# Where TensorE's moving operand lies: high and low parts of the forms apart, or by turns tile by tile

## The reference

```python
z = rmsnorm(x, g_attn) @ w_in                                   # 2048 -> 4608
mix = concat([attention, memory attention, recurrence])          # 2048
x1 = x + mix @ w_out                                             # 2048 -> 2048
up = causal_dwconv3(rmsnorm(x1, g_ffn) @ w_up)                   # 2048 -> 12288
val, gate = split(up)
h = gelu(gate) * val                                             # 6144
y = x1 + h @ w_down                                              # 6144 -> 2048
```

## Time and profile before

| | |
|---|---|
| median of 3 runs | 2290.98 us (2290.85 to 2291.15) |
| the profiled execution, its own time | 2290.06 us |
| its span, first to last instruction | 2288.3 us |
| PE busy, matmuls | 2277.7 us, 17,856 |
| PEld busy | 2259.1 us |
| DVE, ACT, POOL busy | 1854.8, 1187.0, 287.5 us |
| DMA | 309.87 MB, mean 135 GB/s |

### The profile page before, as it was taken

One profiled execution on the slowest core, in us unless ns is written; L12 is line 12 of the kernel. 1 busy time (PEld: TensorE's weight loads), 2 busy tenths in 40 slices (PEclk: granted clock), 3 DMA queues, 4 the chain that ended last, 5 costly groups with the idle time before them and its releaser, 6 DMA issues.

```text
span 2288.3 us, 44911 instructions
## 1 busy us (share of the span) xinstructions
PE 2277.7 (100%) x17856; PEld 2259.1 (99%) x17856; DVE 1854.8 (81%) x2478; ACT 1187.0 (52%) x1911; POOL 287.5 (13%) x241
## 2 busy tenths in 40 slices
PE   9999999999999999999999999999999999999999
PEld 8999999999999999999999999999999999999999
DVE  6788667666888988888888888888888988787876
ACT  4566454444554555455555545555555555454643
POOL 4100000000011011121111111211211110000000
PEclk9999999999999999999999999999999999999999
DMA  9522422323345443444343343433445678686864
GB/s 292 156 76 73 125 85 83 112 80 90 113 145 175 114 122 118 119 128 128 110 136 119 117 138 110 139 117 119 136 120 152 169 199 205 162 209 160 218 145 102
DMA packets 479605, 309.87 MB, mean 135 GB/s; under 512 B 11176, under 2 KB 457640, under 8 KB 479416
## 3 DMA queue, kind: packets, MB, share of 16 engines
q1 hardware_dynamic: 470984, 289.97, 43.1%
q0 software_dynamic: 8432, 17.27, 4.5%
HBM read 255.79 MB, written 53.51 MB: 135 GB/s over the span
## 4 chain that ended last, share of the span: by engine, by line
PE 62%; DVE 2%; issue 1%; ACT 0%; DVEq 0%; ACTq 0%
PE out L2944 21%; PE out L2945 21%; PE out L2946 21%; DVE ring_l L2301 1%; DVE fl L2549 0%; ACT ring_h L1566 0%; DVE pair L2333 0%; DVE s_buf L2313 0%; DVE out L2404 0%; DVE pair L2340 0%; DVE pair L2323 0%; DVE ub L2532 0%; ACT fh L1743 0%; DVE ub L2360 0%; DVE stage L2357 0%
## 5 line engine op out<-in xcount | busy, mean ns | idle before, releaser
L2301 DVE TENSOR_TENSOR ring_l<-pair,ring_h 128x1024 fp32r<-128x1024 f32 (+1 forms) x384 | 455.0, 1185 | 176.2 <-ACT ring_h L1566 176.0
L1566 ACT CAST ring_h<-pair 128x1024 fp32r<-128x1024 f32 (+1 forms) x384 | 383.1, 998 | 323.0 <-DVE pair L2333 227.3
L2944 PE MATMUL out<-t,ring_h 128*128 128x272 f32 x1760 | 507.9, 289 | 2.3 <-DVE ring_l L2301 2.3
L2946 PE MATMUL out<-t,ring_l 128*128 128x272 f32 x1760 | 507.3, 288 | 0.0
L2945 PE MATMUL out<-t,ring_h 128*128 128x272 f32 x1760 | 505.1, 287 | 0.0
L2944 PE MATMUL out<-b,ring_h 128*128 128x272 f32 x1392 | 401.1, 288 | 0.7 <-issue 0.5
L2945 PE MATMUL out<-b,ring_h 128*128 128x272 f32 x1392 | 400.3, 288 | 0.0
L2946 PE MATMUL out<-b,ring_l 128*128 128x272 f32 x1392 | 400.1, 287 | 0.0
L2944 PE MATMUL out<-fh,ring_h 128*128 128x272 f32 x1344 | 387.2, 288 | 2.6 <-DVE ring_l L2301 1.6
L2945 PE MATMUL out<-fl,ring_h 128*128 128x272 f32 x1344 | 386.5, 288 | 0.0
L2946 PE MATMUL out<-fh,ring_l 128*128 128x272 f32 x1344 | 384.2, 286 | 0.0
(11 more groups left out here) (294 smaller groups left out, 3940.9 us busy)
## 6 DMA issues: line engine op xcount, KB each, us to landing
pair<-in_w_up SPq DMA_DIRECT2D x192, 512.0 KB, 4.0
raw<-in_w_in SPq DMA_DIRECT2D x36, 1024.0 KB, 5.7
pair<-in_w_down SPq DMA_DIRECT2D x64, 384.0 KB, 4.7
pair_d<-in_w_down SPq DMA_DIRECT2D x64, 384.0 KB, 4.7
h_forms<-fb SPq DMA_DIRECT2D x24, 816.0 KB, 6.2
fr<-h_forms SPq DMA_DIRECT2D x24, 816.0 KB, 7.4
out_yT<-stage POOLq DMA_DIRECT2D x31, 544.0 KB, 7.9
pair<-in_w_out SPq DMA_DIRECT2D x28, 512.0 KB, 5.0
```

Source lines behind the costliest of these rows:

```text
L1566: nc.scalar.copy(ring_h[:, n % 3, 0:width(i)], weight_of(p, i)).then_inc(op_hi, 1)
L2301: v.tensor_tensor(ring_l[:, n % 3, 0:w], weight_of(p, i), ring_h[:, n % 3, 0:w].bitcast(F32), ALU.subtract).then_inc(op_lo, 1)
L2944: mm(out, w_high, high[:, k, :], start=opens and k == 0, stop=False, skip_group_check=True)
L2946: ins = mm(out, w_low, high[:, k, :], start=False, stop=k == tiles - 1, skip_group_check=True)
```

## The change

The high and the low part of a form of mix or x1 no longer are two arrays; they share one array of 2 x 8,704 bytes in which tile k's high part is followed by tile k's low part. The constants `B_FIRST` and `T_FIRST` are gone, so all forms start at multiples of 256 bytes, and `X_ROOM` shrinks by 192 bytes, which moves `raw`, `wh`, `wl` and the rings behind it by 192 bytes and `overlay`, rounded to 256, by 256. A slot of h now holds, three times over, two high tiles followed by two low tiles. In DRAM the stored forms are arranged in pairs of tiles, so that a load finds 2,176 bytes in a row per partition where it found 1,088, and a store of the six forms of one tile writes six runs of 1,088 bytes per partition where it wrote one of 6,528. In `block`, `tile_of` picks the tile out of either arrangement. Count, order, shape and waits of the instructions stay as they are.

```diff
-B_FIRST = (16, 80, 80, 112, 112, 272)
-T_FIRST = (-112, -16, 48, 112, 112, 112, 128, 320)
-X_ROOM = 320
+X_ROOM = 128
...
         def form_at(name, first):
-            lead = first % 32 // 4
-            t = over(name, [P, lead + K8 * HALF], first - 4 * lead, F32R)
-            return t[:, lead:].rearrange("p (k n) -> p k n", k=K8)
-        b_forms = [form_at(f"b{n}", overlay + n * form + B_FIRST[n]) for n in range(6)]
+            t = over(name, [P, K8, 2, HALF], first, F32R)
+            return t[:, :, 0, :], t[:, :, 1, :]
+        v22, v21, v11 = (form_at(f"b{n}", overlay + 2 * n * form) for n in range(3))
...
-        x_forms = [form_at(f"t{n}", x_at + n * form + T_FIRST[n]) for n in range(8)]
-        v22, v21, v11 = (b_forms[n:n + 2] for n in (0, 2, 4))
-        x_1, x_2, x_3, x_4 = (x_forms[n:n + 2] for n in (0, 2, 4, 6))
+        x_1, x_2, x_3, x_4 = (form_at(f"t{n}", x_at + 2 * n * form) for n in range(4))
...
-        fh = [over(f"fh{n}", [P, K6, HALF], a, F32R) for n, a in enumerate(slot_at)]
-        fl = [over(f"fl{n}", [P, K6, HALF], a + slot_size // 2, F32R) for n, a in enumerate(slot_at)]
-        fr = [over(f"fr{n}", [P, K6, HALF], a + slot_size // 2) for n, a in enumerate(slot_at)]
+        slot_split = [over(f"fs{n}", [P, K6 // 2, 2, 2, HALF], a, F32R) for n, a in enumerate(slot_at)]
+        slot_raw = [over(f"fr{n}", [P, K6 // 2, 2, 2, HALF], a) for n, a in enumerate(slot_at)]
+        fh, fl = ([t[:, :, half] for t in slot_split] for half in range(2))
+        fr = [t[:, :, 1] for t in slot_raw]
...
-        b11_dram = nc.dram_tensor("h_b11", [FT // 2, P, HALF], F32, kind="Internal")
-        fb_dram = nc.dram_tensor("h_forms", [FT // 2, P, 6, HALF], F32, kind="Internal")
+        b11_dram = nc.dram_tensor("h_b11", [FT // 4, P, 2, HALF], F32, kind="Internal")
+        fb_dram = nc.dram_tensor("h_forms", [FT // 4, P, 6, 2, HALF], F32, kind="Internal")
...
-                sp.dma_start(fr[n % SLOTS_D][:], src.rearrange("t p n -> p t n")
+                sp.dma_start(fr[n % SLOTS_D][:], src.rearrange("t p k n -> p t k n")
...
-                sp.dma_start(fb_dram.ap()[i // 2], fb[:]).then_inc(fb_out, 16)
+                sp.dma_start(fb_dram.ap()[i // 4, :, :, i // 2 % 2], fb[:]).then_inc(fb_out, 16)
...
+            def tile_of(form, k):
+                return form[:, k, :] if len(form.shape) == 3 else form[:, k // 2, k % 2, :]
+
             def block(out, slot, high, low, tiles, opens):
                 for k in range(tiles):
                     w_high, w_low = (t[:, slot, k * P:(k + 1) * P] for t in (ring_h, ring_l))
-                    mm(out, w_high, high[:, k, :], start=opens and k == 0, stop=False, skip_group_check=True)
+                    hs, ls = tile_of(high, k), tile_of(low, k)
+                    mm(out, w_high, hs, start=opens and k == 0, stop=False, skip_group_check=True)
...
```

More of the change, by code:

```diff
@@ L268, in form_at @@
         def form_at(name, first):
-            lead = first % 32 // 4
-            t = over(name, [P, lead + K8 * HALF], first - 4 * lead, F32R)
-            return t[:, lead:].rearrange("p (k n) -> p k n", k=K8)
-        assert overlay + 6 * form + B_FIRST[-1] <= nc.sbuf_top, nc.sbuf_top - overlay
-        b_forms = [form_at(f"b{n}", overlay + n * form + B_FIRST[n]) for n in range(6)]
+            t = over(name, [P, K8, 2, HALF], first, F32R)
+            return t[:, :, 0, :], t[:, :, 1, :]
+        assert overlay + 6 * form <= nc.sbuf_top, nc.sbuf_top - overlay
+        v22, v21, v11 = (form_at(f"b{n}", overlay + 2 * n * form) for n in range(3))
         sum1 = rstd[:].rearrange("p c n -> p (c n)")
         sq1 = over("sq1", [P, ROWS], wl_at + 16 * K8 * P - 4 * ROWS)
-        x_forms = [form_at(f"t{n}", x_at + n * form + T_FIRST[n]) for n in range(8)]
-        assert T_FIRST[-1] <= X_ROOM and x_at + T_FIRST[0] >= rows_at + 4 * KT * ROWS
-        assert form + T_FIRST[1] + form <= 4 * K8 * ROWS
-        v22, v21, v11 = (b_forms[n:n + 2] for n in (0, 2, 4))
-        x_1, x_2, x_3, x_4 = (x_forms[n:n + 2] for n in (0, 2, 4, 6))
+        x_1, x_2, x_3, x_4 = (form_at(f"t{n}", x_at + 2 * n * form) for n in range(4))
+        assert 2 * form <= 4 * K8 * ROWS
         mix_form = {1: v11, 2: v21, 3: v22, 5: x_1, 7: x_2, 4: x_3, 6: x_4}
@@ L313, in encoder @@
                    overlay + slot_size + 256, overlay, u_at + 128]
-        assert slot_at[4] >= overlay + 4 * form + B_FIRST[4]
-        fh = [over(f"fh{n}", [P, K6, HALF], a, F32R) for n, a in enumerate(slot_at)]
-        fl = [over(f"fl{n}", [P, K6, HALF], a + slot_size // 2, F32R) for n, a in enumerate(slot_at)]
-        fr = [over(f"fr{n}", [P, K6, HALF], a + slot_size // 2) for n, a in enumerate(slot_at)]
+        assert slot_at[4] >= overlay + 4 * form
+        slot_split = [over(f"fs{n}", [P, K6 // 2, 2, 2, HALF], a, F32R) for n, a in enumerate(slot_at)]
+        slot_raw = [over(f"fr{n}", [P, K6 // 2, 2, 2, HALF], a) for n, a in enumerate(slot_at)]
+        fh, fl = ([t[:, :, half] for t in slot_split] for half in range(2))
+        fr = [t[:, :, 1] for t in slot_raw]
         pair1_d = over("pair1_d", [P, 4, K6 * P], rows_at)
@@ L945, in load_form @@
                 sp.wait_ge(fb_out, 16 * K6 * (c + 1))
-                src = b11_dram.ap()[K6 * c:K6 * (c + 1)] if p == 1 else \
-                    fb_dram.ap()[K6 * c:K6 * (c + 1), :, {2: 0, 3: 1, 5: 2, 6: 3, 7: 4, 4: 5}[p], :]
-                sp.dma_start(fr[n % SLOTS_D][:], src.rearrange("t p n -> p t n")
+                some = slice(K6 // 2 * c, K6 // 2 * (c + 1))
+                src = b11_dram.ap()[some] if p == 1 else \
+                    fb_dram.ap()[some, :, {2: 0, 3: 1, 5: 2, 6: 3, 7: 4, 4: 5}[p]]
+                sp.dma_start(fr[n % SLOTS_D][:], src.rearrange("t p k n -> p t k n")
                              ).then_inc(form_in[n % SLOTS_D], 16)
@@ L952, in store_b11 @@
                 sp.wait_ge(h_ready, i + 1)
-                sp.dma_start(b11_dram.ap()[i // 2], h_even[:, 0:HALF]).then_inc(b11_out, 16)
+                sp.dma_start(b11_dram.ap()[i // 4, :, i // 2 % 2], h_even[:, 0:HALF]).then_inc(b11_out, 16)
             def store_forms(i):
                 sp.wait_ge(t_made, 2 * (i + 1))
-                sp.dma_start(fb_dram.ap()[i // 2], fb[:]).then_inc(fb_out, 16)
+                sp.dma_start(fb_dram.ap()[i // 4, :, :, i // 2 % 2], fb[:]).then_inc(fb_out, 16)
             for g in range(CELLS - 1):
@@ L2943, in block @@
                     w_high, w_low = (t[:, slot, k * P:(k + 1) * P] for t in (ring_h, ring_l))
-                    mm(out, w_high, high[:, k, :], start=opens and k == 0, stop=False, skip_group_check=True)
-                    mm(out, w_high, low[:, k, :], start=False, stop=False, skip_group_check=True)
-                    ins = mm(out, w_low, high[:, k, :], start=False, stop=k == tiles - 1, skip_group_check=True)
+                    hs, ls = tile_of(high, k), tile_of(low, k)
+                    mm(out, w_high, hs, start=opens and k == 0, stop=False, skip_group_check=True)
+                    mm(out, w_high, ls, start=False, stop=False, skip_group_check=True)
+                    ins = mm(out, w_low, hs, start=False, stop=k == tiles - 1, skip_group_check=True)
                 return ins
```

## The result

The changed kernel takes 2298.81 us (median of 7 runs, 2296.76 to 2299.61) against 2290.85 us for the kernel before beside it: a ratio of 1.0032, 95% interval 1.0023 to 1.0042. I had forecast 2285.0 us. It is slower where I expected it faster, and outside the range.

A forecast was written before the change was run, and what follows sets the result against it. PE's matmul stream was taken as the bound, so time follows pitch: -6.6 us for mix and x1 forms, +0.6 for h forms, the rest zero, -6.0 from 2290.98 gives 2285.0 us. Range 2276 to 2297.

The forecast's parts named there:

- Weights and buffers moved by 192 bytes: Shift of weights and rings: taken as zero, with 3.3 us either way allowed on the input projection.
- Term A: Mix and x1 forms, output and up-projection: pitch falls to 124.6 ns, 6.6 us less; bounds 12.0 less to 9.0 more.
- Term B: Down-projection's h forms: pitch goes from 124.44 to 124.6 ns, 0.6 us more; bounds 1.6 less to 6.9 more.
- x_1's 126.3: Up-projection: slowest block pitch in the profile before, in ns, taken as upper bound for the new order of reads.
- The slower rival: All form stages: short read steps collide, 126.3 ns for mix and x1, 125.4 for h; 12.3 us more, 2303; chance 0.19.
- its 0.36 ns: Rise of mean pitch over 12,833 matmuls outside the DVE-led stretches, 4.6 us, at which the slower rival decides.
- What would show it: Signs of being wrong: x1 blocks at 3.01 us or more, down blocks above 2.26; input projection's pitch moving names the weights' shift.
- splits and DMA: ACT's and DVE's gapped writes, and DRAM loads and stores: costed at zero; chance 0.02 that they alone make it slower.
- ACT's wait for a load: ACT waited 1.0 us for a load; earlier loads could give that back at most, taken as zero for PE.
- rule of separate ports: PE's SBUF reads: independent ports, so no address matters and the sum of both pitch terms would be zero.
- The 116 ns of the prediction: Matmul pitch by the skill's formula, 272 / 2.4 + 2.5, an estimate set against the profile's 124.4 to 126.3.

The follow-up runs named there:

- e15: Kernel before with 64 bytes of padding ahead of `wh`, so weights and rings move and all forms and slots stay; 2296.87 us, 1.0024.
- e3: Changed kernel with X_ROOM back at 320, so weights, rings and overlay lie as before; five runs 2288.3 to 2290.1 us, five 2302.9 to 2304.9.
- e13: Kernel of e3 with 64 bytes of padding ahead of `wh`, forms and slots in place; 2298.12 us, 1.0029.
- e12: Kernel of e3 once more without an edit, for a profile of a slow execution; 2303.11 us.
- e9: Changed kernel with X_ROOM 576, rings at 320 modulo 512; same pitches and both groups of times as e3.
- e4: Kernel before with X_ROOM 640, its layouts kept, rings at 384 modulo 512 as in the changed kernel; 2294.95 us, 1.0018.
- e14: Kernel of e3 with 64 bytes of padding between `wh` and `wl`, so only the low weights move; 2298.98 us, 1.0028.

## Why the prediction was wrong

*The step that failed* is "Weights and buffers moved by 192 bytes": "The value I take is zero, in the middle", and with it the bound, which let the shift act on the input projection only. The shift acts on every stage that reads the rings. With no layout touched (e15 and before), by the pitches: input projection 3,456 x 0.43 = 1.5 us (its last matmul starts 1.0 later), up-projection 7,751 x 0.36 = 2.8, down-projection 3,690 x 0.38 = 1.4, output projection about -0.1 (125.35 against 125.45), together 5.6 us; the run gave 5.0. The text had said the reason for doubt itself, that all blocks before have one place of the ring so that no row separates it; that made the term unknown, not small.

*How much of the miss it is.* I forecast -6.0 us, and the changed kernel took 8.0 more than before, 14 us off. With the rings in place the layouts give -2.1 in the quick runs of e3 (median of five 2289.2, before beside it 2291.3), so the sizes of A and B account for some 4 us. The padding (e13, +6.3) takes some 8 from there. The rest, under 2 us, is near what the clock's dips cost. Even with the rings in place 2285 would not have come: half of these runs took 2303 to 2305. That one order of reading has one pitch was a premise of the whole sum, and it is false.

*Term A, mix and x1 forms.* The value of 124.6 holds within 0.22 ns where the rings stay and the quick pattern comes: 7,751 x 0.45 + 1,392 x 0.63 = 4.4 us less, where I had 6.6. With the rings moved it is 125.55, which costs 2.1 us in the up-projection. The bound from x_1's 126.3 was nearly wide enough for the long pattern, 126.67. The reading behind 124.6, starts at multiples of 64 against others, rested on the two ends of the list: before, v22 starts 16 and 80 bytes past a multiple of 256 and has 124.93, and by turns, with every start a multiple of 64, the same forms take 124.82, 125.55 or 126.67.

*Term B, h forms.* Right in sign and bounds, too small: 0.74 ns by the h part alone (2.7 us for the 0.6 I took), 1.12 ns in the changed kernel (3,690 x 1.12 = 4.1 us). The 0.38 between them may be the rings' or the other pattern that e12 has.

*Sum.* In the profiles: input projection, seen as the later start of the output projection, +0.9; output projection nothing; up-projection 2.1 of pitch and 1.5 of the clock's dip; down-projection +4.1; together 8.6 for a span that grew by 8.3.

*The slower rival* had the right sign, and the mean pitch did rise by more than its 0.36 ns (6.3 us over 12,833 matmuls, 0.49 ns), but for the wrong reason: its 125.4 for the h forms was met (125.56), its 126.3 for x1 forms not, and short steps as such aren't bad, since with rings at 256 the h forms in pairs have 124.44. *What would show it* worked: x1 blocks at 3.01 us, the down blocks at 2.26, and the input projection's pitch, which named the weights' shift before any run.

*Right:* no wait added, the gaps kept, splits and DMA nothing for the time, and all of the time in the pitch but for the clock's 1.5. Of the DMAs' landing I had expected too much: stores took 6.4 us and not 7 to 8, loads 7.2 and not 6 to 7. ACT's wait for a load fell from 1.0 to 0.3 us and, as I had put it, gave PE nothing.

*Of the rule of separate ports* (the Trainium skill, "SBUF — State Buffer", section "SBUF: two separate sides", and "TensorE: Matmul & The Clock Gate", section "Step-by-step: what each phase is for"). These pages of the Trainium skill name ports and say nothing of addresses; that the sum would be zero was my reading of them, and the runs here contradict that reading. The place of the weights changes the pitch of matmuls whose moving operand stayed, by 0.4 ns with the old layouts, and for the forms by turns it takes the patterns of 124.82 and 126.67 away and puts 125.55 in their place. Whether the ports are independent no run here shows. The 116 ns of the prediction were misapplied as well: the Trainium skill's section "Back-to-back issue gap" gives that formula for matmuls apart from a stream of weight loads and matmuls, and such a stream is what runs here, at 123.3 to 126.7 ns.

*Open:* by what mechanism the place acts, since nothing in the trace names what a matmul waits for within its 125 ns. The padding moves not only what PE reads but also where ACT and DVE write the weights' parts, and some small tiles behind them; no run separates these. The runs show that place and pattern go together, down to the single step, and that only the remainder modulo 256 counts in e3 and e9, and in e15 and e4. What chooses between two patterns behind a wait wasn't steered, only seen, and no experiment here fixes the choice with the rings at 64.

## What to carry to other kernels

Where a kernel is a stream of matmuls without gaps, a change of addresses is a change of pitch, and every operand that moves counts, the weights that merely shift too: move one thing at a time, and pad so that the rest stays. Look for runs that fall into two groups before trusting a median; here the layout with the better pitch in e3's profile was a coin toss worth 14 us. When no row separates a term, keep it unknown for each stage that it can reach and let the range say so.

## What was unexpected of the hardware

The same matmuls at the same addresses have several steady patterns, each repeating itself over one block or a few: 124.82 and 126.67 ns for forms by turns, 125.18 and 125.56 for h forms in pairs, 123.33 and 125.33 in e14. Where one gave way to another, a gap or a stretched step (135 ns at the least, in e14) stood ahead of it, and a pattern held for up to 970 us. 64 bytes of padding ahead of the weights cost 5.0 us of 2291. And the granted clock fell to 0.50, the 1.2 GHz level, behind a wait of 2.1 us in the changed kernel's profile and not behind the same wait in that of before.
